# Modulation sums turned inside the first FFN's loop, later pieces fetched beside it, final norm summed beside the latent keys

## The chip, the cores and the metric

One core of a Trainium2 chip (trn2) runs the whole program as one launch. The metric is the device time in microseconds; lower is better. Engines are named as in the profile: PE is TensorE, DVE VectorE, ACT ScalarE, POOL GpSimd, SP SyncE, whose queue issues nearly all DMAs.

## The reference

Two transformer-like blocks run one after the other on x, 256 tokens by 1024 features, in float32:

```python
# first block, layer 0: state-space mixer + attention; layer 1: conformer convolution
for layer in range(2):
    mod = silu(c) @ mod_w[layer] + mod_b[layer]         # 6 x 1024 values
    sh1, sc1, g1, sh2, sc2, g2 = split(mod, 6)
    h = modulate(rms_norm(x, norm_g[layer, 0]), sh1, sc1)
    x = x + g1 * mixer(h)      # layer 1: w_in, gate, 31-tap causal conv, layer norm, silu, w_out
    h = modulate(rms_norm(x, norm_g[layer, 1]), sh2, sc2)
    x = x + g2 * ((silu(conv3(h @ w_gate)) * (h @ w_up)) @ w_down)    # hidden 2816
x = rms_norm(x, final_g)
# second block: layer 0 latent attention (queries 512, keys/values 256 latent) over
# ctx and x, layer 1 Hyena; each with its own modulation and an FFN
mod_x = silu(c_2) @ mod_w_2[i] + mod_b_2[i];  mod_c = silu(c_ctx_2) @ mod_w_2[i] + mod_b_2[i]
...
return rms_norm(x, final_g_2)
```

## The kernel before, in words

Features lie on the 128 partitions, tokens along the free axis: x is 8 tiles of 128x256. All projection weights come as a stream of 186 chunks of 1 MB through three buffers (`raw`). A float32 product is made of three fp32r products: ScalarE rounds a chunk to `w_hi` (L653), VectorE forms `w_lo` (L1121), and TensorE multiplies hi by hi, lo by hi and hi by lo (`three`, L1882), 48 records a chunk. A buffer is loaded again when its chunk is split, and split again when TensorE has used the chunk before last. Each engine works through its own list in program order; the order is written out by hand, and semaphores join the lists. SP's list (`load_plain`, `load_ffn`, `load_later`) is one queue too: a load that waits holds up all loads behind it.

The modulation of the second layer of each block is made on VectorE inside an FFN's loop: 16 blocks of 384 columns, each as eight multiply-adds of a weight tile with silu(c) (`mod_block`, L1133). Half-blocks arrive by DMA in six buffers, `mod_w`. The sum of a block is a row for every partition; three products with a column of ones per block (`mod_turn`, L1832, L1837) add over the partitions and turn the result into columns. The blocks are kept in `mod_keep`, and the first FFN's are turned at four places: blocks 2 to 5 behind the loop, 0 and 1 behind the norm's sum, 6 to 10 and 11 to 15 behind the first two pairs of cm_in chunks.

The modulation of the second block's first layer (48 "later pieces" of 512 KB, `mod_later`) is made on TensorE in the conformer stage (`later`, L2143) through six buffers `later_w` that share the memory of the modulation sums and their weights: so the first six are issued only when all sums of the first FFN are made (L511). `later_pieces(p)` tells which pieces stand at which place:

```python
def later_pieces(p):
    return range((0, 0, 9, 18, 29, 40)[p], (0, 9, 18, 29, 40, 48)[p])
```

An FFN (`ffn`) runs its first steps, then five turns of a loop of six chunks each: gate, up, down, gate, up, down. TensorE's products of a turn follow each other; ScalarE and VectorE make the three-tap convolution, silu and product.

The conformer stage has four rounds p. On TensorE a round is two cm_in chunks, then the products of the last taps of round p-1 (`conv_taps`, L2121: PE_TAPS of the 31 taps as products with diagonal matrices that ScalarE makes), then later pieces. On VectorE it is a weight split, the gating of two tiles (L1586), a second split, the other taps of these tiles (L1596, L1606), and the addition of TensorE's taps of round p-1 (`add_taps`, L1573). TensorE can run the chunks of round p+1 as soon as the gating of round p has freed the banks. Then come the mean over the features (L2170), a layer norm and `cm_out`.

A norm (`NORMS`, by number) is: squares on ScalarE (`square`), sums over the partitions on TensorE (`norm_sum`, L1819), a square root (`norm_std`) on ScalarE, a reciprocal (L1272) and scalings on VectorE, rounding on ScalarE (`norm_upper`, L686, L688) and the lower part on VectorE. The second block's first norm uses a shortcut (both gains at once), so the first block's own final norm of x is needed only where x is added to next, behind the attention (`mla_out`). It is number 10 and stands behind the third query chunk (uq): four squares, eight sums in bank 7, root, and on VectorE, behind the rotary products of the queries, the scaling of x (`final_norm`). Numbers 8 and 9 are the norms of the latent keys of ctx and of x.

## Time and profile before

| | us |
|---|---|
| three runs | 1642.93, 1647.58, 1647.23; median 1647.23 |
| the profiled execution | 1644.33, of it the span 1642.6 |
| PE busy | 1529.7 (93%) |
| PE weight loads busy | 1363.5 (83%) |
| DVE busy | 1200.4 (73%) |
| ACT busy | 733.6 (45%) |
| read from memory | 304.17 MB, 186 GB/s over the span |

Busy is the time in which an engine has an instruction under way; matmuls are pipelined, so that records of 0.28 us follow each other every 0.12. The first FFN runs from about 249 to 444 us, the conformer stage to about 608, cm_out to 646, the second FFN to 846, and the latent attention to 1047. A granted clock of 1.00 is 2.4 GHz and one of 0.50 is 1.2 GHz; a value between them is a mean over a stretch with both.

### The profile page before, as it was taken

How to read it: one execution, taken by the hardware profiler on the slowest of the kernel's cores; microseconds unless marked ns; L12 is line 12 of the kernel's file. 1: busy time of each engine (PE TensorE's matmuls, PEld its weight loads, DVE VectorE, ACT ScalarE, POOL GpSimd, SP SyncE). 2: the span in 40 equal slices, each digit the busy share in tenths (PEclk: the TensorE clock that was granted, in tenths of full speed). 3: DMA queues.
4: the chain of work that ended last, by engine and by line, in shares of the span. 5: the costliest groups of instructions: out<-in, count | busy, mean ns of one | idle time of the engine just before them, and what ended most of it. 6: DMA issues, size and time to landing. Idle time of an engine off the chain costs nothing.

```text
span 1642.6 us, 29301 instructions
## 1 busy us (share of the span) xinstructions
PE 1529.7 (93%) x11399; PEld 1363.5 (83%) x11399; DVE 1200.4 (73%) x1902; ACT 733.6 (45%) x977; POOL 52.1 (3%) x38
## 2 busy tenths in 40 slices
PE   4698899999998889999989789999999999999998
PEld 2584489999996658999989666789999787899997
DVE  7999648998987716899985545377666768576665
ACT  2322445444462214544444466455454632365443
POOL 2501100000000000000000000000000000000000
PEclk9698999999999889999999899999999999999999
DMA  8334827888545551988842400225555433245551
GB/s 351 128 103 168 302 95 323 339 306 334 196 171 214 221 227 52 384 331 332 332 163 103 128 13 1 105 103 187 197 179 192 145 125 108 99 154 176 181 181 51
DMA packets 55191, 307.90 MB, mean 187 GB/s; under 512 B 6631, under 2 KB 7688, under 8 KB 30984
## 3 DMA queue, kind: packets, MB, share of 16 engines
q1 hardware_dynamic: 53272, 302.40, 49.8%
q10 hardware_dynamic: 1840, 4.41, 0.9%
q8 instruction: 54, 0.88, 0.2%
q14 instruction: 25, 0.20, 0.0%
HBM read 304.17 MB, written 1.05 MB: 186 GB/s over the span
## 4 chain that ended last, share of the span: by engine, by line
PE 80%; DVE 11%; ACT 3%; issue 3%; DMA 3%; POOL 0%; DVEq 0%; ACTq 0%
PE bank L1882 62%; PE bank L1819 2%; PE bank L2130 2%; DMA arena<-in_mod_later 2%; PE bank L2273 2%; PE bank L2113 2%; PE bank L2239 1%; DVE hf L1289 1%; DVE w_lo L1121 1%; DVE rstd L1272 1%; DVE h_lo L1298 1%; ACT w_hi L653 1%; PE bank L2151 1%; PE bank L1837 1%; PE bank L2257 1%
## 5 line engine op out<-in xcount | busy, mean ns | idle before, releaser
L1882 PE MATMUL bank<-h_hi,w_hi 128*128 128x256 f32 x2184 | 632.2, 289 | 24.3 <-DVE h_lo L1298 19.3
L1882 PE MATMUL bank<-h_lo,w_hi 128*128 128x256 f32 x2184 | 624.2, 286 | 0.0
L1882 PE MATMUL bank<-h_hi,w_lo 128*128 128x256 f32 x2184 | 624.0, 286 | 0.0
L1121 DVE TENSOR_TENSOR w_lo<-raw,w_hi 128x2048 fp32r<-128x2048 f32 x186 | 426.3, 2293 | 139.6 <-ACT w_hi L653 138.4
L1882 PEld LDWEIGHTS bank<-h_hi,w_hi 128*128 128x128 f32 x2184 | 425.7, 195 | 37.9 <-DVE h_lo L1298 24.1
L1882 PEld LDWEIGHTS bank<-h_lo,w_hi 128*128 128x128 f32 x2184 | 425.7, 195 | 1.1 <-issue 0.7
L1882 PEld LDWEIGHTS bank<-h_hi,w_lo 128*128 128x128 f32 x2184 | 425.3, 195 | 0.0
L653 ACT ACTIVATE w_hi<-raw 128x2048 fp32r<-128x2048 f32 x186 | 355.0, 1910 | 134.1 <-PE bank L1882 120.5
L1882 PE MATMUL bank<-a_hi,w_hi 128*128 128x256 f32 (+1 forms) x760 | 220.8, 291 | 4.7 <-DVE a_lo L1487 4.7
L1882 PE MATMUL bank<-a_lo,w_hi 128*128 128x256 f32 (+1 forms) x760 | 219.7, 289 | 0.0
L1882 PE MATMUL bank<-a_hi,w_lo 128*128 128x256 f32 (+1 forms) x760 | 219.6, 289 | 0.0
L1462 DVE SCALAR_TENSOR_TENSOR arena<-bank,par,arena 128x255 f32<-128x255 f32 (+1 forms) x264 | 109.1, 476 | 102.5 <-ACT arena L849 70.7
L1882 PEld LDWEIGHTS bank<-a_hi,w_hi 128*128 128x128 f32 x760 | 148.7, 196 | 7.2 <-DVE w_lo L1121 5.1
L1882 PEld LDWEIGHTS bank<-a_hi,w_lo 128*128 128x128 f32 x760 | 148.7, 196 | 0.7
L1882 PEld LDWEIGHTS bank<-a_lo,w_hi 128*128 128x128 f32 x760 | 148.6, 196 | 0.5
L849 ACT ACTIVATE arena<-bank,par 128x256 f32<-128x256 f32 x88 | 44.8, 560 | 139.3 <-PE bank L1882 139.3
L1154 DVE SCALAR_TENSOR_TENSOR arena<-arena,silu_c 128x384 f32 (+1 forms) x192 | 104.3, 613 | 0.0
L1819 PE MATMUL bank<-sq,ones 128*128 128x256 f32 x208 | 58.2, 429 | 8.7 <-ACT sq L666 7.5
L1606 DVE SCALAR_TENSOR_TENSOR hf<-arena,par,hf 128x256 f32<-128x256 f32 x160 | 64.3, 478 | 0.8 <-DVE hf L1606 0.5
L867 ACT ACTIVATE a_hi<-arena 128x512 fp32r<-128x512 f32 x44 | 27.8, 631 | 79.9 <-DVE arena L1483 79.7
L1819 PEld LDWEIGHTS bank<-sq,ones 128*128 128x128 f32 x208 | 42.7, 217 | 18.9 <-ACT sq L666 9.0
L688 ACT ACTIVATE h_hi<-hf,mod 128x256 fp32r<-128x256 f32 x64 | 31.1, 506 | 53.2 <-DVE hf L1289 53.2
(279 smaller groups left out, 1566.2 us busy)
## 6 DMA issues: line engine op xcount, KB each, us to landing
raw<-in_stream SPq DMA_DIRECT2D x186, 1024.0 KB, 5.0
arena<-in_mod_stream SPq DMA_DIRECT2D x64, 768.0 KB, 6.5
arena<-in_mod_later SPq DMA_DIRECT2D x48, 512.0 KB, 6.9
raw<-in_mod_pe SPq DMA_DIRECT2D x36, 512.0 KB, 6.4
arena<-in_mod_pe SPq DMA_DIRECT2D x12, 512.0 KB, 12.5
sq<-in_bias SPq DMA_DIRECT2D x8, 256.0 KB, 6.8
x<-in_x_t ACTq DMA_DIRECT2D x1, 1024.0 KB, 9.1
arena<-in_ctx_t SPq DMA_DIRECT2D x1, 1024.0 KB, 4.7
```

The source lines that it names most:

```text
L653: nc.scalar.activation(w_hi[s][:], raw[s][:], ACT.Copy).then_inc(hi_done, 1)
L688: ins = nc.scalar.activation(v["parts"][0][:, k, :], hf[:, k, :], ACT.Identity, bias=mod[:, v["l"], v["sh"] + k:v["sh"] + k + 1])
L849: ins = nc.scalar.activation(gate_c[:, e, :], half(4, e), ACT.Identity, scale=par[:, bass.ds(wb[center] + 2 * s + e, 1)], bias=par[:, bass ...
L1121: nc.vector.tensor_tensor(w_lo[s][:], raw[s][:], w_hi[s][:].bitcast(F32), ALU.subtract).then_inc(lo_done, 1)
L1154: ins = nc.vector.scalar_tensor_tensor(parts[e], w, c, parts[e], ALU.mult, ALU.add)
L1462: ins = nc.vector.scalar_tensor_tensor(o, src, par[:, bass.ds(w[tap] + 2 * s + e, 1)], o, ALU.mult, ALU.add)
L1606: chain.on(nc.vector.scalar_tensor_tensor(hf[:, k, :], padded[:, k, bass.ds(tap, T)], par[:, bass.ds(wt + k + DT * tap, 1)], hf[:, k, :], ...
L1819: ins = nc.tensor.matmul(bank[7][:, 0:T], ones[:], sq[:, k, :], start=(k == 0), stop=(k == 2 * pairs - 1))
L1882: ins = nc.tensor.matmul(out_, l, r, start=first and n == 0, stop=last and n == 2, **kw)
L2113: ins = nc.tensor.matmul(bank[2 * part + ft][:], dft[:, part, t, ft * P:(ft + 1) * P], sources[part][:, t, 512 * s_:512 * s_ + 512], start ...
L2130: nc.tensor.matmul(half(p % 3, e), diag[n], padded[:, 2 * p + e, t0:t0 + T], start=(t == 0), stop=(t == PE_TAPS - 1)).then_inc(sem("diag_u ...
L2273: ins = nc.tensor.matmul(bank[4 + kt // 2][:, c:c + P], mla_s(h, t)[:, kt * P:(kt + 1) * P], scaled_ident[2 * (h % 2) + t], start=True, st ...
```

## The change

- The first FFN's sums are no longer kept. VectorE makes each block in its buffer `mod_acc`, and TensorE turns it inside the loop (`mod_turn_now`): block 0 of a turn behind the first down chunk, block 1 ahead of the second, block 2 behind it; block 15 behind the last chunk. The second FFN keeps its sums as before.
- `later_w` moves to the memory that this frees. The first six pieces are issued without a wait behind the first FFN's loads, and used ahead of cm_in; the others are spread anew (8, 8, 8, 10 and 8 at the later places), with SP's order to match: cm_in 5 ahead of pieces 6 to 11, cm_in 6, pieces 12 to 17, cm_in 7.
- PE_TAPS goes from 10 to 8: VectorE takes two more taps of each tile.
- The final norm becomes number 8. ScalarE makes its squares, one by one, into free halves of `hf` and `sq`, behind the squares of the latent queries; TensorE sums them into bank 3 behind the rotary product of the latent key; VectorE scales x ahead of the latent key's norm.

```diff
--- before.py
+++ after.py
@@ -39,7 +39,7 @@
...
 TAPS = 31
-PE_TAPS = 10
+PE_TAPS = 8
...
@@ -299,7 +299,8 @@
...
         diag = [at(FREE - 2 * PE_TAPS * P + i * P, P) for i in range(2 * PE_TAPS)]
-        later_w = [at(i * PM_COLS, PM_COLS) for i in range(LATER_SLOTS)]
+        LATER = FREE + START_SLOTS * HALF
+        later_w = [at(LATER + i * PM_COLS, PM_COLS) for i in range(LATER_SLOTS)]
         later_acc = [at(FREE + START_SLOTS * HALF + MOD_BLOCKS * MOD_COLS + (1 + i) * T, T) for i in range(2)]
...
@@ -356,6 +357,8 @@
...
+        x_squares = [v[:, k, :] for v in (hf, sq) for k in range(4, DT)]
         bank = [ctx.enter_context(nc.psum_tensor(f"bank{i}", [P, 512], F32)) for i in range(8)]
...
@@ -390,7 +393,7 @@
...
         def later_pieces(p):
-            return range((0, 0, 9, 18, 29, 40)[p], (0, 9, 18, 29, 40, 48)[p])
+            return range((0, 6, 14, 22, 30, 40)[p], (6, 14, 22, 30, 40, 48)[p])
...
@@ -456,12 +459,13 @@
...
                  norm_of(c_q, column("mla_g_q_2"), kt=QL // P, width=QL, parts=q_parts)]
+        NORMS.append(norm_of(x, column("final_g"), parts=None))
         for e in range(2):
...
                                  parts=tuple(kv_part(v)[:, :, e, :] for v in (a_hi, a_lo))))
-        NORMS += [norm_of(x, column("final_g"), parts=None), norm_of(x, column("norm_ffn_g_2", 0), 3, 24), norm_of(x, column("norm_mix_g_2", 1), 4, 0),
+        NORMS += [norm_of(x, column("norm_ffn_g_2", 0), 3, 24), norm_of(x, column("norm_mix_g_2", 1), 4, 0),
                   norm_of(x, column("norm_ffn_g_2", 1), 4, 24), norm_of(x, column("final_g_2"), parts=None)]
-        LAYER_NORM, BOTH, FINAL, FINAL_2 = 3, 5, 10, 14
+        LAYER_NORM, BOTH, FINAL, FINAL_2 = 3, 5, 8, 14
         X_HALF = {1: 1, 2: 2, 4: 3, 5: 4, 11: 6, 12: 7, 13: 8, 14: 9}
...
@@ -507,9 +511,7 @@
...
                 for m in range(m0, m1):
-                    if m < LATER_SLOTS:
-                        sp.wait_ge(sem("mod_used"), MOD_SLOTS + 2 * MOD_BLOCKS)
-                    else:
+                    if m >= LATER_SLOTS:
                         sp.wait_ge(sem("later_used"), m - LATER_SLOTS + 1)
...
@@ -573,15 +575,17 @@
...
             load_ffn(0, MB[1])
-            load_plain("cm_in", 0, 2)
             load_later(0, 6)
-            load_plain("cm_in", 2)
+            load_plain("cm_in", 0, 6)
+            load_later(6, 12)
+            load_plain("cm_in", 6, 7)
+            load_later(12, 18)
+            load_plain("cm_in", 7)
+            load_later(18, 20)
             load_plain("cm_out", 0, 1)
-            load_later(6, 9)
-            load_plain("cm_out", 1, 2)
-            load_later(9, 15)
-            load_plain("cm_out", 2, 3)
-            load_later(15, 48)
+            load_later(20, 27)
+            load_plain("cm_out", 1, 3)
+            load_later(27, 48)
             load_plain("cm_out", 3)
...
@@ -674,7 +678,7 @@
...
                     act.wait_ge(sem("rstd_ready"), n)
-                nc.scalar.activation(std[:], bank[7][:, 0:T], ACT.Sqrt, bias=(eps_2 if n == BOTH else eps)[:, 0:1], scale=1.0 / NORMS[n]["width"])\
+                nc.scalar.activation(std[:], bank[3 if n == FINAL else 7][:, 0:T], ACT.Sqrt, bias=(eps_2 if n == BOTH else eps)[:, 0:1], scale=1.0 / NORMS[n]["width"])\
                     .then_inc(sem("std_ready"), 1)
...
@@ -966,6 +970,9 @@
...
                 square(7, p)
+            act.wait_ge(sem("h_ready"), H[7])
+            for k in range(DT):
+                nc.scalar.activation(x_squares[k], x[:, k, :], ACT.Square).then_inc(sem("sq_ready"), 1)
             act.wait_ge(chunk_done, Q["dkv"] + 1)
...
@@ -976,7 +983,9 @@
...
             hi_upto(Q["dkv"] + 4)
-            latent_norm(8)
+            square(9, 0)
+            norm_std(FINAL)
+            latent_norm(9, squared=True)
...
@@ -1001,14 +1010,10 @@
...
                 if c == 0:
-                    square(9, 0)
+                    square(10, 0)
                 hi_upto(Q["uq"] + c + 3)
                 if c == 1:
-                    latent_norm(9, squared=True)
-            for p in range(DT // 2):
-                square(FINAL, p)
-            norm_std(FINAL)
+                    latent_norm(10, squared=True)
             def kv_ready(n):
...
@@ -1134,8 +1139,13 @@
...
                 part = mod_acc[b % len(mod_acc)]
-                k0 = b % MOD_BLOCKS * MOD_COLS
-                parts = [mod_keep[:, bass.ds(k0 + 3 * MOD_COLS * per, MOD_COLS)], part[:, 1, :]]
+                if b < MOD_BLOCKS:
+                    if b >= len(mod_acc):
+                        dve.wait_ge(sem("mod_turned"), b - len(mod_acc) + 1 + 3 * per)
+                    parts = [part[:, 0, :], part[:, 1, :]]
+                else:
+                    k0 = b % MOD_BLOCKS * MOD_COLS
+                    parts = [mod_keep[:, bass.ds(k0 + 3 * MOD_COLS * per, MOD_COLS)], part[:, 1, :]]
                 last = [None, None]
...
@@ -1565,7 +1575,7 @@
...
-            mod_out(1, 6, "mod_b", 0, 18)
+            mod_out(1, 16, "mod_b")
             norm(2)
...
@@ -1610,8 +1620,6 @@
...
                     add_taps(p - 1)
-                if p == 1:
-                    mod_out(1, 16, "mod_b", 18, 48, 2)
             add_taps(3)
...
@@ -1654,11 +1662,13 @@
...
-            norm(8)
+            final_norm(FINAL)
+            dve.wait_ge(sem("x_ready"), 12)
+            norm(9)
             for c in range(3):
...
                 if c == 1:
-                    norm(9)
+                    norm(10)
...
@@ -1668,7 +1678,6 @@
...
             nc.vector.tensor_tensor(q_p, q_p, q_raw, ALU.add).then_inc(sem("q_pe_ready"), 1)
-            final_norm(FINAL)
             lo_upto(Q["ukv"] + 4)
...
@@ -1706,7 +1715,6 @@
...
             mla_lower(MH // 2 - 1)
-            dve.wait_ge(sem("x_ready"), 12)
             add_to_x("mla_out", 3, 16)
...
@@ -1816,7 +1824,8 @@
...
                     pe.wait_ge(sem("sq_ready"), 2 * SQ[n] + k + 1)
-                    ins = nc.tensor.matmul(bank[7][:, 0:T], ones[:], sq[:, k, :], start=(k == 0), stop=(k == 2 * pairs - 1))
+                    dst, src = (bank[3], x_squares[k]) if n == FINAL else (bank[7], sq[:, k, :])
+                    ins = nc.tensor.matmul(dst[:, 0:T], ones[:], src, start=(k == 0), stop=(k == 2 * pairs - 1))
                 if p == pairs - 1:
...
@@ -1836,6 +1845,14 @@
...
                     ins.then_inc(sem("mod_turned"), 1)
+            def mod_turn_now(b, column, i=None):
+                pe.wait_ge(sem("mod_used"), MOD_SLOTS + 2 * b + 2 + (0 if i is None else 6 * i))
+                for n in range(3):
+                    ins = nc.tensor.matmul(bank[6][:, bass.ds(column + n, 1)], mod_acc[b % len(mod_acc)][:, 0, n * P:(n + 1) * P],
+                                           ones[:, 0:1], start=True, stop=True)
+                ins.then_inc(sem("mod_turned"), 1)
...
@@ -2098,10 +2115,14 @@
...
                         up_gate(s, q, i)
+                        if b0 is not None and e:
+                            mod_turn_now(b0 + 1, 9 * i + 3, i)
                         down(s - 1, q + 2, i)
-                if f == 0:
-                    mod_turn(b0, range(2, 6))
+                        if b0 is not None:
+                            mod_turn_now(b0 + 2 * e, 9 * i + 6 * e, i)
                 down(10, q0 + 32, last=True)
+                if b0 is not None:
+                    mod_turn_now(b0 + 15, 45)
...
@@ -2116,7 +2137,6 @@
...
             norm_sum(2)
-            mod_turn(MB[1], (0, 1))
             stay_awake(12)
...
@@ -2159,8 +2179,6 @@
...
                     conv_taps(p - 1)
-                if p < 2:
-                    mod_turn(MB[1], range(6 + 5 * p, 11 + 5 * p), 2)
                 if p:
...
@@ -2202,12 +2220,12 @@
...
             nc.tensor.matmul(bank[2][:, 0:T], turn_w, k_pe[:, 1, :], start=True, stop=True).then_inc(sem("k_turned"), 1)
-            norm_sum(8)
+            norm_sum(FINAL)
+            norm_sum(9)
             for c in range(3):
...
                 if c == 1:
-                    norm_sum(9)
-            norm_sum(FINAL)
+                    norm_sum(10)
             pe.wait_ge(bank_free, FILL["uq"] + 6)
...
```

## Rows read from the trace of the kernel before

**Rows 1.** By stretch: us; busy PE, PEld, DVE, ACT, POOL; clock; DMA share; GB/s
```profile
265.00:437.00 172.00, 171.40 (x1432) 171.35 (x1431) 161.95 (x228) 80.73 (x72) 0.00 (x0) 1.00 0.82 319
466.00:484.00 18.00, 18.00 (x129) 18.00 (x129) 15.55 (x35) 10.40 (x24) 0.00 (x0) 0.81 0.34 129
516.38:547.10 30.72, 27.38 (x218) 22.86 (x217) 22.77 (x48) 11.22 (x25) 0.00 (x0) 0.94 0.53 189
```

**Rows 2.** Chain of waits, 249 to 941 us: start, duration, what (x matmul records)
```profile
by line: PE bank L1882 62.3%; issue 2.9%; PE bank L1819 2.3%; PE bank L2130 2.2%; DMA arena<-in_mod_later 2.0%; PE bank L2273 1.9%; PE bank L2113 1.7%; PE bank L2239 1.5%; DVE hf L1289 1.4%; DVE w_lo L1121 1.3%; DVE rstd L1272 1.2%; DVE h_l
...
249.16 167.31 PE bank L1882 x1392
...
440.20 0.39 issue
...
484.25 8.63 PE bank L2130 x40
492.88 3.32 PE bank L1837 x30
...
507.31 12.72 PE bank L1882 x96
...
581.58 1.48 PE bank L2151 x24
...
593.28 6.15 PE bank L2170 x16
...
934.46 6.27 PE bank L1819 x16
```

**Rows 3.** VectorE in time, last turns of the first FFN's loop: start, duration, instructions
```profile
371.93 1.65 DVE L1462 SCALAR_TENSOR_TENSOR arena<-bank,par,arena 128x255 f32<-128x255 f32 x4 [2.10 <-ACT arena L849]
...
379.73 0.56 DVE L1161 TENSOR_TENSOR arena<-arena 128x384 f32 x1
...
398.23 0.56 DVE L1161 TENSOR_TENSOR arena<-arena 128x384 f32 x1
...
406.49 1.65 DVE L1462 SCALAR_TENSOR_TENSOR arena<-bank,par,arena 128x255 f32<-128x255 f32 x4 [2.09 <-ACT arena L849]
```

**Rows 4.** TensorE in time, 433 to 904 us
```profile
433.57 2.73 PE L1837 MATMUL bank<-ones,arena 128*128 128x1 f32 x24
...
449.76 2.75 PE L1830 MATMUL bank<-zeros 128*128 128x512 bf16 x12
...
502.88 0.64 PE L2151 MATMUL bank<-arena 128*32 128x256 f32 x8 [1.26 <-DMA arena<-in_mod_later]
...
902.28 1.22 PE L2204 MATMUL bank<-arena 128*128 128x256 f32 x2 [1.40 <-ACT arena L954]
```

**Rows 5.** ScalarE in time, first taps of a step in the loop
```profile
370.72 1.02 ACT L849 ACTIVATE arena<-bank,par 128x256 f32<-128x256 f32 x2 [3.43 <-PE bank L1882]
```

**Rows 6.** The turning line L1837: duration in ns min/median/max, first and last start
```profile
L1837 PEld LDWEIGHTS bank<-ones,arena x192: 187/192/339, 433.5 to 900.6; 128*128 128x128 f32 x192
L1837 PE MATMUL bank<-ones,arena x192: 164/250/354, 433.6 to 900.6; 128*128 128x1 f32 x192
```

**Rows 7.** VectorE in time, conformer stage: gating, first taps, forty taps
```profile
467.24 0.88 DVE L1586 SCALAR_TENSOR_TENSOR arena<-bank,par,arena 128x256 f32<-128x256 f32 x2 [2.32 <-ACT arena L920]
...
471.25 0.73 DVE L1596 TENSOR_SCALAR hf<-arena,par 128x256 f32<-128x256 f32 x2
...
525.64 16.06 DVE L1606 SCALAR_TENSOR_TENSOR hf<-arena,par,hf 128x256 f32<-128x256 f32 x40
```

**Rows 8.** ScalarE in time, latent queries and keys
```profile
890.20 1.09 ACT L954 ACTIVATE arena<-bank 128x512 f32<-128x512 f32 x2 [9.97 <-PE bank L1882]
...
914.06 2.42 ACT L991 ACTIVATE arena<-bank 64x512 f32<-64x512 f32 x4 [3.04 <-PE bank L1882]
...
931.03 1.07 ACT L954 ACTIVATE arena<-bank 128x512 f32<-128x512 f32 x2
```

**Rows 9.** VectorE in time, latent key's norm
```profile
907.91 1.75 DVE L1272 RECIPROCAL rstd<-std 128x256 f32<-128x256 f32 x1
```

## The prediction

> **What bounds the kernel now.** The page comes first: its busy shares put TensorE far ahead of every other engine, but a share is an average over stages. So the table by stretches comes next: in the first FFN's loop (265 to 437 us) TensorE works 171.40 of 172 us at granted clock 1.00 and VectorE 161.95; in a round of the conformer stage (516.38 to 547.10) TensorE works 27.38 of 30.72 and VectorE 22.86, and neither is full [rows 1]. The chain of waits says what fills the difference: beside the main matmul line's 62.3%, transfers of the later pieces hold 2.0% of the span, 33 us, all between 499 and 606 us [rows 2]. So the loop is TensorE's own time, where an added matmul costs in full, and the conformer stage is TensorE waiting in its own program order for pieces that nobody needs before the stage ends.
>
> **The loop of the first FFN (added cost).** Turning a block's sums is three products, each of which shows as two matmul records. 30 records took 3.32 us [rows 2], so a block's 6 cost 0.66 us and the three blocks of a loop turn 2.0. A turn is now 34.56 us (between the same VectorE taps), of which VectorE idles 2.10 [rows 3]. TensorE has no slack, so a turn becomes 36.6. From the taps at 406.49, in the last turn, VectorE runs on almost without a gap until it has added to x, so only the four turns before count: 4 x 2.0 = +8.0 us. The turned products of blocks 2 to 5 behind the loop (2.73 us [rows 4]) stood beside that VectorE chain; dropping them gains nothing.
>
> Each turned block adds a wait for its sum, and behind it on TensorE stands the next chunk. A chunk takes 5.77 us (167.31 us for 1392 records, 48 a chunk [rows 2]); the gate chunk ends at 370.7 [rows 5]. Two chunks later, at 382.2, the first block is wanted, done at 380.3; five chunks later, at 399.5, the third, done at 398.8 [rows 3] (the second lies between, with more room). The slacks of 1.9 and 0.7 us only grow as TensorE gets later, so the waits cost nothing. The computed column addresses add instructions to TensorE's queue, and the trace has no such matmul. Below nothing they cannot go; above, I bound each of the 45 by the 0.39 us that a computed address left between VectorE's operations in the same sums [rows 2], 18 us in all. I take 0, by the nearest row on this engine: the 1392 records pass four ends of turns without a gap [rows 2].
>
> A rule of the Trainium skill speaks against me here. A turning record's load lasts 0.19 us and its matmul 0.25, yet the records follow each other every 0.11 [rows 2, 6]: load and matmul overlap. "TensorE: Matmul & The Clock Gate", Part 3, The mechanism, says that a weight load overlaps matmuls in flight only when it goes to another row group, and these loads fill all rows. By that the 72 records would cost 72 x 0.44 = 32 us instead of 8.0. The trace disagrees.
>
> **From the loop to the second chunk of cm_in.** The zero matmuls before cm_in start at 449.76, behind 12 turning records (1.3 us), and last 2.75 [rows 4]. VectorE, which waited for those turned blocks, is spared about a microsecond, but TensorE becomes the later one: it now does six later pieces there. 24 records, three pieces, took 1.48 us [rows 2], so 3.0. It reaches cm_in at 449.76 - 1.3 + 8.0 + 2.75 + 3.0 + about 0.5 for opening the banks = 462.7. The two chunks then run in 11.5 and end at 474.2; today they end at 466.3, a little ahead of the gating [rows 7]. That is +7.9 us. The six pieces' transfers now go out behind the last modulation halves, ahead of cm_in 0: 3 MB at the loop's 319 GB/s [rows 1] are 10 us, which the last two chunks of the loop and the eleven microseconds of VectorE's tail just hide. If not, 1 to 3 us.
>
> **The conformer stage (gain).** I write it in the old clock, from the second chunk's end at 466.3. VectorE's round is 22.86 us of work [rows 1]; the two taps that TensorE gives up are four operations of 16.06/40 = 0.40 us [rows 7] more, 24.5. TensorE's round: two chunks 11.5; 16 products instead of 20 at 8.63/20 = 0.43 [rows 2], 6.9; no turning of modulation; eight pieces. Six of these wait in their buffers, two are fetched as the first are used. In the old block, begun at 493 + 3.3 = 496.2, the second late piece could start at 502.88 [rows 4], 6.7 us in. With the turn of a group's sums inside that wait I take 7.0 for the block; the old one took until 507.31 [rows 2], 11.1. TensorE's round is then 25.4: the engines are about even, where the old round was 30.7.
>
> Sum: chunks 2 and 3 wait for the gating, over at 468.1 [rows 7], and end at 479.7. Products to 486.6, pieces to 493.6; VectorE, whose taps start at 471.3 [rows 7] and last 18.7, has gated at 493.2. Chunks to 505.1. Second round: products 512.0, pieces 519.0, chunks 530.5. Third: 537.4 and 544.4, last products 551.3, then ten pieces, four fetched late (9.5), 560.8, and the eight products of the mean 3.5: 564.3. VectorE's last addition comes at 490.0 + 3 x 24.5 - 2.3 (one split less) + 0.7 = 562. The old mean ended at 593.28 + 6.15 = 599.43 [rows 2]. That is at full clock; where TensorE had waited or turned, two chunks took 12.72 instead of 11.5 [rows 2], and with that in each round and a slow end it is 569. I take 567: -32.4, with the +7.9 **-24.5 us**. The last eight pieces and what follows are unchanged. Bounds 564 to 577 (blocks of 9 to 10 us).
>
> The queue: pieces 6 to 11 stand behind cm_in 5, whose buffer is free once chunk 2 is split, before 466; they are wanted at 486.6. cm_in 7 stands behind pieces 12 to 17 and goes out near 492; with 4 MB in front it lands near 502 and VectorE wants it after its second round's taps, near 515. Both are covered.
>
> **The final norm.** Behind the query chunks go the sums of 6.27 us from 934.46 [rows 2]. The rotary products after them could start when the last queries are evacuated, 931.03 + 1.07 = 932.1 [rows 8], instead of 940.7: up to -8.6. Ahead of the latent keys' norm, ScalarE's eight squares lie in its wait of 9.97 us [rows 8], free. TensorE's eight products begin behind the rotary product of k, at 903.5 [rows 4], and take 3.5 to 6.3; VectorE then does a reciprocal of 1.75 [rows 9] and eight scalings at 0.40 before the key norm. That norm's reciprocal moves from 907.9 [rows 9] to between 913.4 and 915, its upper parts end 3.1 later, ScalarE issues two DMAs (1.4), and evacuates the first queries at 918 to 919.5 instead of 914.06 [rows 8]: +3.9 to +5.4, and all up to 932.1 follows. Net -3.2 to -4.7; a slow clock, which the removed sums bore (0.78 a product instead of 0.43), now meets the rotary products and the first key chunk, +1 to +2. I take **-2.5 us**, bounds -6 and +2.
>
> Together -27.0. The profiled execution took 1644.33 (span 1642.6): 1617.3. The median of the runs is 2.9 above it: **1620 us**.
>
> **Rivals.**
> 1. The pieces stay on the path. For: 6.7 us for two late ones leaves TensorE two idle microseconds a round already, and a 1 MB chunk now goes out among them; against: a third late piece is what made the old blocks 11 us. Blocks of 9 to 10 us, mean at 577, result 1630. 14%.
> 2. Slower: short bursts of turning in the loop bring the clock down. For: with a burst at its start the stretch from 466 had a granted clock of 0.81, partly 1.2 GHz, worth 18 x 0.19 = 3.4 us [rows 1]; against: that burst was 30 records, a block has 6. At 3.4 us for each of 15 blocks, 51 us: 1671. It decides from 27/15 = 1.8 us a block. 4%.
> 3. Turning does not overlap in the loop: 72 x (0.44 - 0.11) = 24 us more, 1644, no change. 2%. (The rule of the sentence above; the trace speaks against it.)
> 4. Half of it: the clock falls in every round and VectorE waits for splits held up by cm_in 7, 10 us less gain, and the final norm costs 2.5 instead: 1635. 8%.
> The forecast holds 72%; its own range is 1611 to 1627.
>
> **Numbers.** Faster by over 0.3% (about what a measurement of this kernel can tell from no change; below 1642.3) 0.93, within 0.3% 0.03, slower 0.04. The range 1607 to 1636 takes in the bounds above and rivals 1 and 4.
>
> **What would show it.** Right: a loop turn of 36.5 to 36.7 us; the pieces' transfers under 15 us in the chain; rounds of 25 to 27 us; the first queries evacuated 4 to 5 us later after dkv and the rotary products 3 to 5 us earlier. Wrong: clock under 0.97 in the loop, turns over 38 us, or blocks of pieces over 9 us.

## The result, and the profile after

The kernel after takes 1626.12 us (median of 4 runs, 1621.31 to 1627.27), the kernel before 1647.4 beside it: ratio 0.9869, interval 0.9841 to 0.9897. Timed again in five rounds with the experiments it gave 1624.81, ratio 0.9867 (0.9843 to 0.9891). So the change makes the kernel faster by 21 to 22 us; the forecast was 1620, a gain of 27. The profiled execution took 1621.31 us (span 1619.5, clock 0.97), 23.0 less than the profiled one of before.

By stretch: us, then busy time (records) of TensorE, weight loads, VectorE, ScalarE, GpSimd, granted clock, DMA share, GB/s. The first three answer to [rows 1]; the third is now one round of the conformer stage, 24.91 us long.

```profile
265.00:437.00 172.00, 170.66 (x1417) 170.46 (x1416) 151.85 (x210) 76.18 (x70) 0.00 (x0) 0.99 0.84 321
466.00:484.00 18.00, 16.07 (x140) 15.35 (x134) 12.78 (x20) 12.84 (x21) 0.00 (x0) 1.00 0.49 187
505.54:530.45 24.91, 23.60 (x202) 20.17 (x201) 24.62 (x52) 9.62 (x21) 0.00 (x0) 1.00 0.65 254
...
275.00:285.00 10.00, 8.66 (x62) 8.46 (x62) 9.97 (x14) 4.35 (x3) 0.00 (x0) 0.85 1.02 420
...
915.00:920.00 5.00, 5.00 (x12) 3.95 (x13) 3.43 (x2) 1.51 (x1) 0.00 (x0) 0.50 0.11 16
```

In a round VectorE is now busy 24.62 of 24.91 us and TensorE 23.60: both are nearly full, where before neither was. The fourth row is the loop's first turn, where the clock fell; the fifth the rotary products, at 1.2 GHz throughout.

The chain of waits (start, duration, what; L1853 turns a block, L1899 is the main matmul line, L2171 the later pieces, L2150 the taps), against [rows 2]:

```profile
281.96 13.10 PE bank L1899 x96
...
393.01 11.61 PE bank L1899 x96
404.62 0.56 PE bank L1853 x6
...
428.96 0.56 PE bank L1853 x6
429.53 10.53 PE bank L1899 x87
...
505.54 11.70 PE bank L1899 x96
517.24 6.91 PE bank L2150 x32
524.15 1.04 PE bank L2171 x16
525.21 4.55 DMA arena<-in_mod_later
...
529.81 0.64 PE bank L2171 x8
530.45 11.70 PE bank L1899 x96
```

From 393.01 to 429.53 is one turn of the loop, 36.52 us, with three blocks of 0.56. A round's block of eight pieces lasts 6.30 us (524.15 to 530.45), with one late transfer in it. The first turn has a wait that I had not foreseen (TensorE in time, the wait ahead of it in brackets):

```profile
281.13 0.82 PE L1853 MATMUL bank<-ones,arena 128*128 128x1 f32 x6 [1.34 <-DVE arena L1171]
```

And the latent part of the chain, behind the final norm's reciprocal (L1571 scales x, L2232 is the rotary products):

```profile
887.79 0.62 DVE x L1571 x2
...
888.59 2.47 DVE x L1571 x6
891.09 1.76 DVE rstd L1282
...
896.57 7.44 PE bank L1899 x48
...
918.55 12.50 PE bank L1899 x48
```

```profile
914.77 3.78 PE L2232 MATMUL bank<-arena 128*128 128x256 f32 x8 [3.41 <-ACT arena L958]
```

The scaling of x stands on the chain, ahead of the key norm's reciprocal at 891.09. The second query chunk (896.57) takes 7.44 us behind a wait of 4.08, before 6.00 behind one of 1.38. The rotary products (TensorE in time, second fence) come behind 3.41 us of idling and take 3.78 us, before 1.73; the key chunk takes 12.50, before 11.63.

### The profile page after: what moved, and what is told of

Same layout as the page of the kernel before. It is cut to its first block, busy times and chain, and to the rows that moved or that the text cites. A ratio compares the mean times of both kernels' runs of the same rounds, so it can differ in the third digit from the quotient of the medians.

```text
span 1619.5 us, 29310 instructions
## 1 busy us (share of the span) xinstructions
PE 1508.7 (93%) x11352; PEld 1349.4 (83%) x11367; DVE 1206.9 (75%) x1917; ACT 728.7 (45%) x965; POOL 52.1 (3%) x38
## 4 chain that ended last, share of the span: by engine, by line
PE 79%; DVE 11%; ACT 4%; DMA 3%; issue 3%; ACTq 0%; POOL 0%; DVEq 0%; SPq 0%
PE bank L1899 62%; PE bank L1828 2%; PE bank L2291 2%; PE bank L2150 2%; PE bank L2134 2%; DMA arena<-in_mod_later 2%; PE bank L2257 2%; DVE hf L1299 2%; DVE rstd L1282 1%; DVE h_lo L1308 1%; ACT w_hi L657 1%; DVE w_lo L1126 1%; PE bank L2275 1%; DMA raw<-in_stream 1%; PE bank L1967 1%
## 5 line engine op out<-in xcount | busy, mean ns | idle before, releaser
L1899 PE MATMUL bank<-h_hi,w_hi 128*128 128x256 f32 x2184 | 630.5, 289 | 33.1 <-DVE h_lo L1308 23.4
L1899 PE MATMUL bank<-h_lo,w_hi 128*128 128x256 f32 x2184 | 622.7, 285 | 0.0
L1899 PE MATMUL bank<-h_hi,w_lo 128*128 128x256 f32 x2184 | 622.6, 285 | 0.0
L1126 DVE TENSOR_TENSOR w_lo<-raw,w_hi 128x2048 fp32r<-128x2048 f32 x186 | 426.4, 2294 | 135.7 <-ACT w_hi L657 134.8
L1899 PEld LDWEIGHTS bank<-h_hi,w_hi 128*128 128x128 f32 x2184 | 423.9, 194 | 39.5 <-DVE h_lo L1308 22.0
L1899 PEld LDWEIGHTS bank<-h_lo,w_hi 128*128 128x128 f32 x2184 | 423.9, 194 | 1.1 <-issue 0.7
L1899 PEld LDWEIGHTS bank<-h_hi,w_lo 128*128 128x128 f32 x2184 | 423.9, 194 | 0.0
L1899 PE MATMUL bank<-a_hi,w_hi 128*128 128x256 f32 (+1 forms) x760 | 220.9, 291 | 5.4 <-DVE a_lo L1497 5.4
L1899 PE MATMUL bank<-a_lo,w_hi 128*128 128x256 f32 (+1 forms) x760 | 219.0, 288 | 0.0
L1899 PE MATMUL bank<-a_hi,w_lo 128*128 128x256 f32 (+1 forms) x760 | 218.6, 288 | 0.0
L1899 PEld LDWEIGHTS bank<-a_hi,w_hi 128*128 128x128 f32 x760 | 147.9, 195 | 8.1 <-DVE w_lo L1126 5.8
L1899 PEld LDWEIGHTS bank<-a_hi,w_lo 128*128 128x128 f32 x760 | 148.0, 195 | 0.8
L1899 PEld LDWEIGHTS bank<-a_lo,w_hi 128*128 128x128 f32 x760 | 148.0, 195 | 0.6
L1164 DVE SCALAR_TENSOR_TENSOR arena<-arena,silu_c 128x384 f32<-128x384 f32 (+1 forms) x192 | 104.3, 612 | 0.0
L1616 DVE SCALAR_TENSOR_TENSOR hf<-arena,par,hf 128x256 f32<-128x256 f32 x176 | 70.6, 479 | 1.1 <-DVE hf L1616 0.4
L871 ACT ACTIVATE a_hi<-arena 128x512 fp32r<-128x512 f32 x44 | 27.8, 631 | 72.5 <-DVE arena L1493 72.4
L1828 PE MATMUL bank<-sq,ones 128*128 128x256 f32 x200 | 52.6, 408 | 1.8 <-ACT sq L675 1.0
L1282 DVE RECIPROCAL rstd<-std 128x256 f32<-128x256 f32 x15 | 26.3, 1752 | 32.4 <-ACT std L681 32.3
```

The source lines that it names most:

```text
L1126: nc.vector.tensor_tensor(w_lo[s][:], raw[s][:], w_hi[s][:].bitcast(F32), ALU.subtract).then_inc(lo_done, 1)
L1164: ins = nc.vector.scalar_tensor_tensor(parts[e], w, c, parts[e], ALU.mult, ALU.add)
L1282: nc.vector.reciprocal(rstd[:], std[:]).then_inc(sem("rstd_ready"), 1)
L1616: chain.on(nc.vector.scalar_tensor_tensor(hf[:, k, :], padded[:, k, bass.ds(tap, T)], par[:, bass.ds(wt + k + DT * tap, 1)], hf[:, k, :], ...
L1828: ins = nc.tensor.matmul(dst[:, 0:T], ones[:], src, start=(k == 0), stop=(k == 2 * pairs - 1))
L1899: ins = nc.tensor.matmul(out_, l, r, start=first and n == 0, stop=last and n == 2, **kw)
```

## The experiments

Executions of the same code differ by up to 3.5 us within a stage (130.3 and 133.9 for after), so I compare them by three stretches of their traces: the **loop**, from VectorE's reciprocal ahead of the first FFN to the first chunk of cm_in; the **stage**, from there to the first chunk of cm_out; and the **latent** part, from the first chunk of latent keys to ScalarE's split of the second chunk of key and value weights. Each is a difference of two starts in the chain of waits (us):

| kernel | loop | stage | latent | median | ratio to before |
|---|---|---|---|---|---|
| before | 209.0 | 165.3 | 73.1 | 1647.4 | 1 |
| after | 220.0 | 130.3 | 72.5 | 1626.12 | 0.9869 |
| after, again | 220.6 | 133.9 | 72.0 | 1624.81 | 0.9867 (0.9843 to 0.9891) |
| turning only | 219.6 | 155.6 | 73.2 | 1648.59 | 1.0017 (1.0003 to 1.0031) |
| ten taps | 220.6 | 137.9 | 72.2 | 1627.68 | 0.9890 (0.9870 to 0.9909) |
| first block late | 220.4 | 134.8 | 72.5 | 1625.18 | 0.9876 (0.9857 to 0.9895) |
| eight buffers | 220.4 | 124.5 | 72.2 | 1614.90 | 0.9814 (0.9798 to 0.9830) |
| order alone | 220.6 | 131.0 | 72.7 | 1621.90 | 0.9855 (0.9832 to 0.9879) |
| ten buffers | 220.4 | 123.1 | 72.2 | 1616.26 | 0.9831 (0.9816 to 0.9847) |
| norm back | 220.3 | 133.0 | 72.6 | 1624.46 | 0.9892 (0.9874 to 0.9911) |
| zeros | 220.3 | 134.9 | 69.4 | 1619.84 | 0.9844 (0.9821 to 0.9867) |
| scaling late | 220.4 | 131.1 | 69.0 | 1615.09 | 0.9828 (0.9812 to 0.9844) |
| all together | 220.3 | 125.9 | 65.3 | 1608.54 | 0.9775 (0.9755 to 0.9795) |

### The turning alone

The kernel before, with TensorE's turning in the loop, straight from VectorE's sums in `mod_acc`, and nothing else of the change (SyncE's first six pieces wait for the last turned block):

```
                         up_gate(s, q, i)
+                        if b0 is not None and e:
+                            mod_turn_now(b0 + 1, 9 * i + 3, i)
                         down(s - 1, q + 2, i)
+                        if b0 is not None:
+                            mod_turn_now(b0 + 2 * e, 9 * i + 6 * e, i)
...
-                if p < 2:
-                    mod_turn(MB[1], range(6 + 5 * p, 11 + 5 * p), 2)
```

> The kernel before, with one part of the change alone: the second modulation vector's sums are turned inside the first FFN's loop. The later pieces keep their old buffers and are fetched after the last turned block, ten taps a chunk stay on TensorE, the final norm stands at its old place. Theory (the sum of the forecast, corrected by the trace after): the loop pays 8 to 11 us; the rounds of the convolution lose the turned groups of products (two groups of ten columns, about 3.6 us each), and the step of 1.2 us behind the second chunk: 0 to +3 us against the kernel before, about 1648 to 1650. So the turning alone brings nothing; it is what makes room for the early fetch. Rival: the gain of the change comes from the turning itself and from TensorE's clock, which fell right behind each group of turned columns: then this kernel is 5 to 12 us faster than before.

Ratio 1.0017: 2.8 us slower at the median, in the profiles 1.4. The loop pays 10.6 us, the stage gives 9.7 back. So the turning by itself brings nothing, and the gain lies in the rest of the change, for which it makes room. The rival falls. The long late transfers are still there (the chain, start, duration, what):

```profile
502.62 8.00 DMA arena<-in_mod_later
...
567.10 6.92 DMA arena<-in_mod_later
```

### Ten taps on TensorE

```
-PE_TAPS = 8
+PE_TAPS = 10
```

> The kernel after, with ten of the convolution's taps a chunk on TensorE, as before, in place of eight. Theory: with the pieces' wait gone, VectorE's 44 products (17.8 us) fill a round of 24.9 us of which TensorE's products, pieces and chunks take nearly all too; two taps less a chunk take VectorE down to about 23 us, but TensorE's round goes up to about 26.6: 1.7 us a round, 5 to 7 us slower than the kernel after (1631 to 1633 at its median of 1626). Rival: VectorE alone sets the rounds, and two taps less on it make the kernel 4 to 6 us faster than after.

3.5 to 3.8 us slower than after by the ratios (0.0021 to 0.0023 of 1646), the intervals overlapping; the stage is 4 to 7.6 us longer than in the two executions of after. A round (509.31 to 535.91) is 26.6 us, as expected for TensorE, so the rival (VectorE alone sets the rounds) falls. The whole is 1 to 3.5 us cheaper than expected.

```profile
509.31 11.71 PE bank L1899 x96
521.02 8.64 PE bank L2150 x40
...
535.91 11.71 PE bank L1899 x96
```

### The first block turned later

Only the first of three blocks moves, from behind the turn's first down chunk to behind its second up chunk; the third stays behind the second down chunk, where it was.

```
                         if b0 is not None and e:
+                            mod_turn_now(b0, 9 * i, i)
                             mod_turn_now(b0 + 1, 9 * i + 3, i)
                         down(s - 1, q + 2, i)
-                        if b0 is not None:
-                            mod_turn_now(b0 + 2 * e, 9 * i + 6 * e, i)
+                        if b0 is not None and e:
+                            mod_turn_now(b0 + 2, 9 * i + 6, i)
```

> The kernel after, with the first of the three blocks' sums turned behind the second up chunk (beside the second one's) and the third behind the second down chunk, so that each is turned some 10 us after its sum is done. Theory: in the first turn of the loop TensorE waited 1.34 us for the first sum and its clock fell right behind the wait (0.86 from 278 to 290); both go, the loop costs 8.0 us as forecast instead of 10.9, and the kernel is 2.9 us faster than after. Rival: the clock falls there for another reason, for example the turned columns alone: 1.3 us faster. Second rival: the wait is only moved to the products behind it, which wait for the late weights anyway: no change.

No change: loop 220.4 us, ratio 0.9876. The first block's wait is gone (12 records at 290.57, no bracket), and the clock stays at 1.00 up to 295. But VectorE is late through the whole first turn (a weight transfer of 13.30 us is in its chain, from 258.55), and the third block now has the wait that the first lost; the clock falls right behind it (second fence, 295 to 305 us).

```profile
290.57 1.39 PE L1853 MATMUL bank<-ones,arena 128*128 128x1 f32 x12
298.90 0.82 PE L1853 MATMUL bank<-ones,arena 128*128 128x1 f32 x6 [1.09 <-DVE arena L1171]
```

```profile
295.00:305.00 10.00, 8.86 (x61) 8.58 (x60) 9.33 (x11) 2.43 (x2) 0.00 (x0) 0.83 0.77 252
```

In both kernels the fall stands behind a wait of little over 1 us for a sum. A kernel without any such wait was not tried, and such a wait alone does not bring the fall. In the second profile of after TensorE waits 1.40 us at the same place and the clock stays at 1.00; the 96 records behind it take 11.62 us:

```profile
280.03 0.82 PE L1853 MATMUL bank<-ones,arena 128*128 128x1 f32 x6 [1.40 <-DVE arena L1171]
274.00:284.00 10.00, 8.60 (x72) 8.40 (x71) 9.97 (x14) 4.35 (x3) 0.00 (x0) 1.00 1.01 417
```

With SyncE's order changed it is the same (wait 1.43, 11.62 us). In both of these the sixteen sums ahead of cm_in took 5.41 us in place of 3.72, so the three stretches of the table do not tell the two cases apart. What decides where the clock falls is open.

### After again, and SyncE's order alone

> The kernel after, unchanged, timed again in five rounds beside the others, since its own ratio (0.9869, 0.9841 to 0.9897) is from four runs and the variants differ from it by a few tenths of a per cent. Expected: 0.987 within 0.002, that is 1623 to 1626 us.

> The kernel after with its six buffers, and one change of order on SyncE's queue: the stage's last chunk of weights (eighth of cm_in) is issued ahead of the six pieces behind which it stood. Theory: in four of six traces with this order (the kernels with the final norm back, with the turning late, with the zeros, with eight buffers) the second round's chain runs over this chunk's transfer (13.1 to 13.9 us) and the stage takes 2 to 4.5 us longer than in the trace after (132.96, 134.84, 134.85 against 130.33); issued first, it never comes late, and the kernel is 2 to 4 us faster than the kernel after at the median. Rival: what makes those stages longer is the lower clock in their second chunk (13.2 us in place of 11.75), and the order changes nothing: within 1 us of the kernel after.

```
-            load_later(12, 18)
             load_plain("cm_in", 7)
-            load_later(18, 20)
+            load_later(12, 20)
```

The second profile of after is the more usual one. Its second pair of chunks takes 13.23 us (11.75 in the first), and a chunk of weights comes late: its transfer, its split, ScalarE's diagonals, and only then the copy that TensorE waits for. It is not the eighth of cm_in, as the expectation above has it, but the first of cm_out. SyncE issues cm_in 7 at 504.90, two pieces at 505.34 and this chunk at 506.81, so moving cm_in 7 takes 1 MB out of the queue right ahead of it.

```profile
479.72 13.23 PE bank L1899 x96
...
506.81 13.57 DMA raw<-in_stream
520.40 1.91 ACT w_hi L657
522.31 4.67 ACT arena L933 x16
526.99 0.28 ACT arena L913
...
532.73 11.69 PE bank L1899 x96
```

With the order changed the clock falls there all the same (13.24 us), but cm_out's transfer is gone from the chain and the stage takes 131.0 us in place of 133.9:

```profile
480.98 13.24 PE bank L1898 x96
...
532.19 11.70 PE bank L1898 x96
```

From 479.72 to 532.73 are 53.0 us, from 480.98 to 532.19 51.2: the difference is 1.8 us, and 1.4 more go with the clock (after's first profile has 49.8, and no slow chunk). In all eight traces that fetch cm_in 7 behind the six pieces, ScalarE waits 0.74 to 1.92 us for cm_out's chunk; with cm_in 7 fetched early it does not wait. But in three of the eight (after's first among them) the transfer is off the chain even so. The medians differ by 2.9 us, with overlapping intervals: the mechanism is seen, the size is not settled.

### Eight and ten buffers

```
-LATER_SLOTS = 6
+LATER_SLOTS = 8
-        later_w = [at(LATER + i * PM_COLS, PM_COLS) for i in range(LATER_SLOTS)]
+        later_w = [at(LATER + i * PM_COLS if i < 6 else (i - 6) * PM_COLS, PM_COLS) for i in range(LATER_SLOTS)]
```

The ranges that SyncE loads shift by two pieces; the two new buffers lie where the loop's modulation halves were. The second kernel has ten, loads pieces 6 to 9 behind the third cm_in chunk, and issues cm_in 7 ahead of pieces 16 on.

> The kernel after, with eight buffers for later pieces in place of six, so that no piece of the first three rounds is fetched late. Theory: the block of pieces in each round (6.3 us, one transfer of 4.5 us in its chain) shortens to about 5 us, but VectorE's products fill the round nearly as well, so 0.5 us a round comes back and up to 1 us at each of the two last blocks: 1 to 4 us faster than after. Rival: the late transfers on the chain cost nothing, VectorE sets the rounds: within 1 us of after. A second rival: they are what sets each round: 4 x 1.3 = 5 us faster.

> The kernel after, with ten buffers for later pieces (the four new ones in the first FFN's freed modulation buffers) and SyncE's order changed with them: four more pieces are fetched behind the third chunk of the stage, while the DMA engines are at a third of their time, and the last chunk of weights is issued ahead of the pieces instead of behind them. Theory: with eight buffers the rounds did not shorten (25.8 us each against 24.9) since the chunk of weights came late behind more pieces (13.9 us in the chain), and the gain of 5.8 us came at the two last blocks alone; with ten buffers and the other order the rounds fall back to 24.9 or less and the last block waits for no piece: 2 to 4 us faster than with eight buffers, 8 to 10 us than the kernel after. Rival: VectorE's products set the rounds and the two last blocks wait for VectorE's last addition (it ended the sum's wait at 573.46 with eight buffers): no faster than eight buffers. Second rival: the pieces' traffic now collides with the chunks' and delays the first round: as the kernel after.

Eight buffers gave 9 us (0.9814 against 0.9867, intervals apart), about twice what any theory had. The rounds kept 25.9 us, between the 24.9 and 26.5 of after's two profiles. The gain is behind them (TensorE in time, eight buffers; then the lines of after's first profile):

```profile
564.68 3.23 PE L2173 MATMUL bank<-arena 128*32 128x256 f32 x56
569.24 0.64 PE L2173 MATMUL bank<-arena 128*32 128x256 f32 x8 [1.33 <-DMA arena<-in_mod_later]
...
573.46 1.99 PE L2190 MATMUL bank<-hf,ones 128*128 128x256 f32 x8 [1.66 <-DVE hf L1589]
...
581.73 3.70 PE L1830 MATMUL bank<-sq,ones 128*128 128x256 f32 x16
```

```profile
570.35 0.64 PE L2171 MATMUL bank<-arena 128*32 128x256 f32 x8 [1.69 <-DMA arena<-in_mod_later]
...
572.19 5.38 PE L2188 MATMUL bank<-hf,ones 128*128 128x256 f32 x16
...
582.93 0.64 PE L2171 MATMUL bank<-arena 128*32 128x256 f32 x8 [2.29 <-DMA arena<-in_mod_later]
...
585.78 5.39 PE L1828 MATMUL bank<-sq,ones 128*128 128x256 f32 x16
```

Against the second profile of after, the stage's 9.3 us divide so: 1.3 up to the fourth pair of chunks, 1.4 from there to the last taps' end, 1.6 in the block of ten pieces and the mean, 2.4 in the block of eight, and 2.6 in the layer norm's sixteen products (L1830), which run at the higher clock (3.57 us in place of 6.17). Read so, part of a late transfer's price is the lower clock of what comes after it; that it is the transfer that lowers the clock is argued.

With ten buffers the last two blocks wait for no piece any more, and the stage is shorter by 1.4 us again (less than two executions of after differ by), but not the median (1616.26 against 1614.90, ratios overlapping). The profile of ten buffers is of its fastest execution, 1608.92 us. What is left is VectorE, as the rival said: TensorE waits for its last addition.

```profile
568.51 1.99 PE L2190 MATMUL bank<-hf,ones 128*128 128x256 f32 x8
573.26 1.99 PE L2190 MATMUL bank<-hf,ones 128*128 128x256 f32 x8 [2.76 <-DVE hf L1589]
```

### The final norm: back, its scaling late, and zeros in the waits

The first kernel puts squares, sum, root and scaling where they were. The second leaves the early sum, root and reciprocal, and moves the scaling:

```
-            final_norm(FINAL)
-            dve.wait_ge(sem("x_ready"), 12)
+            dve.wait_ge(sem("std_ready"), FINAL + 1)
+            nc.vector.reciprocal(rstd_x[:], std[:]).then_inc(sem("rstd_ready"), 1)
             norm(9)
...
             nc.vector.tensor_tensor(q_p, q_p, q_raw, ALU.add).then_inc(sem("q_pe_ready"), 1)
+            for k in range(DT):
+                ins = nc.vector.scalar_tensor_tensor(x[:, k, :], x[:, k, :], NORMS[FINAL]["g"](k), rstd_x[:], ALU.mult, ALU.mult)
```

The third adds `awake(12)`, twelve products of zeros, ahead of the second query chunk and ahead of the rotary products.

> The kernel after, with the final norm of the first output at its old place, behind the latent norms. Theory of the trace after: summing it early gains 3.6 us up to the rotary products, of which the lower clock behind them takes back 2.9 (rotary products 3.78 us in place of 1.73, the key chunk 12.50 in place of 11.63), so this kernel is 0.7 us slower than the kernel after. Rival, the forecast: the lower clock is an accident of one execution and the early sum is worth 2.5 to 3.6 us. Second rival: the early scaling of x (3.3 us on VectorE ahead of the second latent norm) costs more than it gains: this kernel is up to 2 us faster.

> The kernel after, with the final norm's sum, root and reciprocal early as there, but the scaling of x by it (eight instructions of VectorE, 3.26 us in the chain ahead of the second latent norm) put behind the rotary queries, where VectorE idles until the key and value weights. The reciprocal goes to a tile of its own. Theory: the scaling is on the chain that ends last, so the whole 3.3 us come back, less up to 1 us of clock: 2 to 3.3 us faster than the kernel after. Rival: VectorE is not what ends the wait there, TensorE's sums for the latent norm or ScalarE's copies are: no change. Second rival: the earlier rotary products come at a lower clock, which takes the gain back, as it did with the early norm: within 1 us.

> The kernel after, with twelve products of zeros on TensorE in each of two waits of the latent stage: ahead of the second chunk of queries (idle until 896.57, the chunk took 7.44 us) and ahead of the rotary products (idle 3.4 us until 914.77, the products took 3.78 us in place of 1.73). Theory: TensorE's clock falls since it sits idle in these waits; twelve products of 0.21 us each fit into them, the chunk takes 6 us, the rotary products 1.75 and the key chunk 11.6: 3 to 4 us faster than the kernel after. Rival: the clock falls for another reason or at another place all the same: within 1 us of the kernel after.

Norm back: latent part 72.6 us against 72.5 and 72.0. The early norm is worth 0.1 to 0.6 us there; in the ratio nothing can be told (0.9892 against 0.9867, intervals overlapping). Its rotary products run fast again, but behind the old sum:

```profile
914.31 6.06 PE bank L1823 x16
920.37 1.73 PE bank L2227 x8
```

Scaling late: 69.0, so -3.0 to -3.5, the size of the first theory, but not by its path alone. Between the two reciprocals the chain is 2.7 us shorter. The sixteen sums ahead of them took 5.97 us in place of 4.36, so the second query chunk starts only 1.1 earlier; it then takes 6.00 in place of 7.44, and the rotary products 2.76 in place of 3.78. So some 0.9 us of the gain over the first profile of after is clock. Its ratio (0.9828) lies 6 us under that of after; the stretch explains half, and where the rest comes from is open. Zeros: 69.4, -2.6 to -3.1. The ratio lies 4 us under that of after, intervals overlapping. The query chunk still took 7.50 us (TensorE idled 2.39 behind the zeros), but the products and the chunk behind the second wait ran at or near full speed:

```profile
918.43 1.99 PE bank L2240 x8
920.43 11.63 PE bank L1904 x48
```

The rotary products took 3.78 us in both profiles of after and 1.99 in both kernels with zeros, so the lower clock there does come from the wait. "TensorE: Matmul & The Clock Gate" of the Trainium skill, section "Why this matters for your kernels", advises against idle gaps between bursts of matmuls; this pair of traces agrees, with 3.78 us behind 3.41 of idling and 1.99 where zeros filled it.

### All together

Ten buffers, late scaling and zeros in one kernel, no edit that the ones above don't have.

> The kernel after with the three gains together: ten buffers for later pieces and the other order of SyncE, the scaling of x behind the rotary queries, and the zeros in two waits of the latent stage. Theory: they lie at different places of the one chain and add up: stage of the convolution 123.1 us in place of 130.3 (-7.2), the stretch from the first chunk of latent keys to the second chunk of keys and values 72.45 - 3.5 - 3.1 = 65.9: 13.8 us less, 1610 us at the median, ratio 0.977 to 0.980. Rival: with the scaling gone from it, the wait ahead of the queries' second chunk is shorter than the twelve zeros (2.6 us), which then stand on the chain: the stretch stays at 69, ratio 0.980 to 0.983.

1608.54 us, ratio 0.9775 (0.9755 to 0.9795): below both kernels, 15 us under after. The stage takes 125.9 us and not 123.1: behind a wait of 4.86 us for VectorE the mean's second eight records took 3.78 us in place of 1.99. The latent part is 65.3 us (65.9 expected). That the sum came out is in part luck: against scaling late, 2.1 of the 3.7 us come from sums that ran faster here, and they stand ahead of all the zeros. The zeros ahead of the second query chunk do stand on the chain now, and end just when it could start; it takes 5.77 us (6.00 without them in scaling late):

```profile
887.38 2.61 PE bank L1854 x12
889.98 5.77 PE bank L1914 x48
...
906.51 1.99 PE bank L2250 x8
908.50 11.64 PE bank L1914 x48
```

## Why the prediction was nearly right

**The loop: +8.0, measured +10.9** (the taps ahead of the last turn's tail at 419.00 against 406.49, less the 1.57 us by which the two executions differed before the change is reached). The turn itself was right (36.52 against 36.6; so the computed addresses cost nothing that shows), the waits were not. I took the slacks, 1.9 and 0.7 us, from a late turn [rows 3] and said they only grow. In the first turn VectorE starts behind weights that land late: TensorE waited 1.34 us, and at the lower clock behind it 96 records took 13.10 us in place of 11.6. That is the missing 2.9. The wait, 1.26 to 1.75 us, is in all eleven traces that turn the block there, the slow records in nine. In the other two (after's second profile and the changed order) the same sum gives +9.5, and the slow stretch comes with the norm's sums ahead of cm_in. So the table's first column rises by 10.6 to 11.6 us in every kernel (all but turning only also have the six pieces ahead of cm_in in it), where my sum had 8.4.

**To the second chunk: +7.9, measured +10.8**: the same 2.9. The six pieces took the 2.73 us I had for them (3.0), and their transfers were in time.

**The stage: -32.4, measured -34.2** (98.9 us from the second chunk to the mean; before 133.1). Rounds 24.9 us (25.4), products 6.91 (6.9), blocks of pieces 6.3 (7.0). In the second profile of after it is 101.4, and -31.7. One sign I named failed: the pieces' transfers hold 24.7 us in the chain, not under 15. The chain follows whatever lands last, and with six buffers two pieces a round are still fetched inside the block; what shortened is the block (11.1 to 6.3), not the transfers' part in it. I had called cm_in 7 covered, and it is: it goes out at 504.32 (492 in the old clock, as I had it), is split at 513.25, and VectorE comes to it at 526.73. What I left out is the chunk behind it, the first of cm_out. ScalarE must split it (519.01 in the first profile, 520.40 in the second) before it makes its diagonals and the copy for TensorE. In the first profile that stays off the chain; in the second, and in four of the variants, it does not.

**The final norm: -2.5, measured -0.7 (-1.1 in the second profile): the step that failed.** Its other parts were about right: first queries evacuated 3.6 us later (3.9 to 5.4), rotary products 3.6 earlier (3.2 to 4.7). The price of the clock was mis-sized: 1 to 2 us, measured 2.9 (2.05 in the rotary products, 0.87 in the key chunk), and 1.4 more in the second query chunk, which I had left at its old length. It was more since the sums that used to fill TensorE's wait were gone and TensorE came to the products from idling; with the norm back all three ran as before (6.00, 1.73 and 11.62 us). And I priced the eight scalings correctly without asking whether they have to be there; late, they leave the chain.

**The sum.** -27.0 became -23.1 in span: 2.9 from the loop and 1.8 from the norm lost, 1.8 more won in the stage; the last 1.0 lies in stretches that the change doesn't touch, where the two executions were 1.57 apart before it is reached. That the sum came within 4 us is thus in part luck, errors of both signs. The median gained less, 21 to 22; a likely reason is that the first profile is of the fastest of the four executions. Of eight traces with six buffers six have the slow second pair, and four cm_out's late chunk in the chain. Rival 1 (pieces stay on the path, 1630) fell by its own condition, blocks of 9 to 10 us (6.3 measured), but part of it holds: at the two last blocks pieces are late, and two buffers more gave 9 us. Rival 2's mechanism, the clock falling in the loop, happened once or not at all in an execution, not fifteen times. Rival 3 fell: 6 records take 0.56 us, so the load does overlap the matmuls, against the words on what overlaps in Part 3, "The mechanism", of the Trainium skill's "TensorE: Matmul & The Clock Gate"; the trace decides. (The same section also lets a load go ahead when it goes to a background weight buffer; my forecast left that out, and no trace here tells which of the two it is.)

## What to carry to other kernels

Read slack from the first turn of a loop, not from a settled one: where an engine starts behind late data, an added wait is paid there, and often again in the clock behind it. A prefetch is worth what the last blocks lack: count which transfers are late at the end of a stage, and price with each the slower products that follow it. When work moves to an earlier place, ask which part of it has to be there; here the sum could go early and the scaling could not.

## What the runs showed of the hardware

Waits of 1.09 and 1.34 us were each followed by a stretch at a lower granted clock (0.83 and 0.85 over 10 us), yet waits of 1.40 and 1.43 us at the place of the second were not, nor was one of 2.76 us ahead of the mean's second half (8 records in 1.99 us; 3.78 behind one of 4.86). Which wait brings the clock down differs between executions of the same code: behind the same wait of 1.93 us the second pair of chunks took 11.75 us in one profile of after and 13.23 in the other. A profile alone can't size an effect under 3 us here.
